# A four-layer encoder trunk: loading the memory in four parts, later placement of two waiting steps, and a last unit stored by token tile

## The reference, cut to what matters

```python
mem_n = rmsnorm(mem, mem_norm)                    # mem, x: 256 x 1024
for i in range(4):                                # kinds: SSM, DIFF, SGU, SSM
    h = rmsnorm(x, norm_mix[i])
    proj = h @ w_in[i]                            # last 1024 columns are the queries xq
    mix_out = mixer_i(proj[..., :-1024])          # mamba2 / differential attention / spatial gating
    k, v = split(mem_n @ w_mem_kv[i], 2)
    cross = softmax(rmsnorm_heads(xq) @ rmsnorm_heads(k).T / 16) @ v
    x = x + concat([mix_out, cross]) @ w_out[i]
    x = x + square(relu(rmsnorm(x, norm_ffn[i]) @ w_ff1[i])) @ w_ff2[i]
return x                                          # 256 x 1024
```

## Time and profile before

| what | value |
|---|---|
| median of 3 runs | 1874.03 us (1873.33 to 1874.39) |
| the profiled execution, its own time | 1873.39 us |
| its span in the profile | 1871.6 us |
| busy: PE, DVE, ACT, POOL | 1819.8, 1122.0, 1005.7, 241.3 us |
| mean granted TensorE clock | 0.99 |
| read from memory | 302.91 MB |

### The profile page before, as it was taken

The page is one execution under the profiler, slowest core; times in us unless marked ns, Lnnn a source line. Parts: engine busy times, 40 slices in busy tenths (PEclk is TensorE's granted clock), DMA queues, the critical chain, the costliest instruction groups (busy, mean ns, idle before and its releaser), DMA issues.

```text
span 1871.6 us, 27875 instructions
## 1 busy us (share of the span) xinstructions
PE 1819.8 (97%) x10596; PEld 1597.1 (85%) x10596; DVE 1122.0 (60%) x1492; ACT 1005.7 (54%) x1613; POOL 241.3 (13%) x581
## 2 busy tenths in 40 slices
PE   6999999999997899999999999999999999999998
PEld 5998878899986678899988888999799897889997
DVE  4877765565554575555556545555577776556554
ACT  5665765454454476454455655444555676545443
POOL 2132340000001131000002300000022144000000
PEclk8999999999998899999999999999999999999999
DMA  6444434555553343555556435555444444355553
GB/s 222 159 146 147 147 113 136 180 191 191 186 177 134 107 147 119 173 188 181 190 180 220 151 125 180 194 188 191 154 160 160 136 148 135 113 183 180 189 191 125
DMA packets 84161, 305.78 MB, mean 163 GB/s; under 512 B 9280, under 2 KB 9664, under 8 KB 84032
## 3 DMA queue, kind: packets, MB, share of 16 engines
q1 hardware_dynamic: 83744, 302.95, 48.7%
q10 hardware_dynamic: 288, 1.05, 0.1%
HBM read 302.91 MB, written 1.05 MB: 162 GB/s over the span
## 4 chain that ended last, share of the span: by engine, by line
PE 64%; DVE 2%; issue 2%; POOL 1%; ACT 1%; DVEq 0%; ACTq 0%
PE ps L1057 13%; PE ps L1059 12%; PE ps L1058 12%; PE ps L1066 6%; PE ps L1067 6%; PE ps L1068 6%; PE ps L1192 1%; PE ps L1212 1%; PE ps L1091 1%; PE ps L1083 1%; PE ps L1142 1%; DVE nt L1510 1%; PE ps L1120 1%; ACT nt L1305 0%; PE ps L1201 0%
## 5 line engine op out<-in xcount | busy, mean ns | idle before, releaser
L1453 DVE TENSOR_TENSOR w_lo_t<-raw,w_hi_t 128x1024 fp32r<-128x1024 f32 x570 | 704.2, 1239 | 514.8 <-ACT w_hi_t L1237 514.1
L1237 ACT ACTIVATE w_hi_t<-raw 128x1024 fp32r<-128x1024 f32 x570 | 601.6, 1060 | 433.8 <-PE ps L1059 200.8
L1066 PE MATMUL ps<-hT_hi,w_hi_t 128*128 128x256 f32 x1536 | 437.8, 285 | 0.0
L1068 PE MATMUL ps<-hT_hi,w_lo_t 128*128 128x256 f32 x1536 | 434.6, 283 | 0.0
L1067 PE MATMUL ps<-hT_lo,w_hi_t 128*128 128x256 f32 x1536 | 434.5, 283 | 0.0
L1057 PE MATMUL ps<-w_hi_t,act_hi 128*128 128x512 f32 x832 | 327.7, 394 | 0.0
L1058 PE MATMUL ps<-w_lo_t,act_hi 128*128 128x512 f32 x832 | 324.1, 390 | 0.0
L1059 PE MATMUL ps<-w_hi_t,act_lo 128*128 128x512 f32 x832 | 324.0, 389 | 0.0
L1067 PEld LDWEIGHTS ps<-hT_lo,w_hi_t 128*128 128x128 f32 x1536 | 294.6, 192 | 1.3
L1066 PEld LDWEIGHTS ps<-hT_hi,w_hi_t 128*128 128x128 f32 x1536 | 294.5, 192 | 1.4
L1068 PEld LDWEIGHTS ps<-hT_hi,w_lo_t 128*128 128x128 f32 x1536 | 294.5, 192 | 0.0
(11 more groups left out here) (191 smaller groups left out, 1967.9 us busy)
## 6 DMA issues: line engine op xcount, KB each, us to landing
raw<-in_wstream SPq DMA_DIRECT2D x570, 512.0 KB, 3.4
mix<-in_mem SPq DMA_DIRECT2D x1, 1024.0 KB, 5.2
x<-in_x SPq DMA_DIRECT2D x1, 1024.0 KB, 10.2
out<-x SPq DMA_DIRECT2D x2, 512.0 KB, 2.8
wsT<-in_sgu_wT ACTq DMA_DIRECT2D x1, 512.0 KB, 4.4
sgain<-in_sgu_gain ACTq DMA_DIRECT2D x1, 512.0 KB, 5.2
consts_sb<-in_consts SPq DMA_DIRECT2D x1, 384.0 KB, 11.2
percol_sb<-in_percol SPq DMA_DIRECT2D x1, 225.5 KB, 6.1
```

The costliest lines, as they stand in the source:

```text
L1066: pe.matmul(o, wh[:, n], ah, start=first and c == 0 and f % 2 == 0, stop=False, skip_group_check=True)
L1068: mm = pe.matmul(o, wl[:, n], ah, start=False, stop=last and c == UK - 1, skip_group_check=True)
L1237: act.activation(w_hi_t[:, u % RING, :], raw[:, u % RING, :], ACT.Copy).then_inc(w_hi, 1)
L1453: dve.tensor_tensor(w_lo_t[:, u % RING, :], raw[:, u % RING, :], w_hi_t[:, u % RING, :].bitcast(F32), ALU.subtract)\
```

## The change

The memory is loaded in four parts of 256 columns (each with a semaphore), issued between the first units; the gain of the memory's norm has a transfer of its own, and the rest of the per-column constants follows behind unit 3 in two transfers, which `setup` now waits for. In the planner the sums of squares and `rms` of the memory stand ahead of unit 0, and `x_norm` holds the sums of x and places `xn` 2 units after `rms`, and the turns 2 units after `xn`. `row_norm` places `nt_turn` 2 units after `norm_mul`. The last unit's `x_add` waits for each token tile by itself, and each is stored by itself (256 KB).

```diff
@@ row_norm
             self.step("norm_mul", job=job, groups=groups, r=r, n=n)
-            yield 1
+            yield 2
             for m in range(2):
                 tj = self.misc_job(True, False)
                 self.step("nt_turn", ...)
@@ build
-        def start():
-            yield 1
-            for nb in range(2):
-                self.sum_squares("mem", nb)
-            yield 1
-            self.r_m = self.rms("mem")
-            self.sum_squares("x", 0)
-            yield 1
-            self.sum_squares("x", 1)
-            yield 1
+        for nb in range(2):
+            self.sum_squares("mem", nb)
+        self.r_m = self.rms("mem")
+        def start():
+            yield 2
             yield from self.x_norm(0)
@@ x_norm
+        for nb in range(2):
+            self.sum_squares("x", nb, self.x_halves[nb])
         r = self.rms("x")
         n = self.count("xn")
-        yield 1
+        yield 2
         self.step("xn", n=n, rms=r)
-        yield 1
+        yield 2
@@ sync
+            mem_part(0)
             sp.dma_start(consts[:, 0:P], A["consts"][:, 0:P]).then_inc(ident_in, 16)
-            sp.dma_start(mix[:, :, D:2 * D], m_in).then_inc(mem_in, 16)
-            sp.dma_start(raw[:, 0, :], A["wstream"][0]).then_inc(raw_in[0], 16)
-            sp.dma_start(pc[:, :], A["percol"]).then_inc(pc_in, 16)
-            for u in range(1, RING):
-                sp.dma_start(raw[:, u, :], A["wstream"][u]).then_inc(raw_in[u], 16)
+            sp.dma_start(pc[:, g], A["percol"][:, g]).then_inc(gain_in, 16)
+            weights(0)
+            mem_part(1)
+            weights(1)
+            mem_part(2)
+            mem_part(3)
+            weights(2)
             sp.dma_start(x[:, :, :], x_rows).then_inc(x_in, 16)
+            weights(3)
+            sp.dma_start(pc[:, 0:g.start], ...).then_inc(pc_in, 16)
+            sp.dma_start(pc[:, g.stop:NPC], ...).then_inc(pc_in, 16)
...
+            for t in range(TT):
+                sp.wait_ge(tail_added, t + 1)
+                sp.dma_start(x_out[:, t, half:D], x[:, t, half:D]).then_inc(stored, 16)
@@ scalar and vector
+                if k == "setup":
+                    act.wait_ge(pc_in, 32)        # vector: the same wait
@@ vector, x_norm step
+                    if n:
+                        dve.wait_ge(x_pn, n)
@@ vector, x_add of the last unit
+                        if tail and t == 0:
+                            dve.wait_ge(tail_done, 1)
+                        elif tail:
+                            dve.wait_ge(job_done, job.done)
```

More of the change, by code:

```diff
@@ L342, in build @@
     def build(self):
-        self.turning, self.ready, self.v_act = False, {}, {}
+        self.turning, self.ready, self.v_act, self.x_halves = False, {}, {}, (0, 0)
         self.parts["mem"] = []
         for m in range(4):
-            self.parts["mem"].append(self.turn("mem", m, "memT", (2 * m, 2 * m + 1), (2 * m, 2 * m + 1), ("mem_norm", 2 * m), ("mem_in", 16)))
+            self.parts["mem"].append(self.turn("mem", m, "memT", (2 * m, 2 * m + 1), (2 * m, 2 * m + 1), ("mem_norm", 2 * m), (f"mem_in{m}", 16)))
             self.steps[-1]["w"] = m - AHEAD + 1
         self.step("setup")
+        for nb in range(2):
+            self.sum_squares("mem", nb)
+        self.r_m = self.rms("mem")
         def start():
-            yield 1
-            for nb in range(2):
-                self.sum_squares("mem", nb)
-            yield 1
-            self.r_m = self.rms("mem")
-            self.sum_squares("x", 0)
-            yield 1
-            self.sum_squares("x", 1)
-            yield 1
+            yield 2
             yield from self.x_norm(0)
-        self.r_m = 1
         self.spawn(start())
@@ L408, in into_x @@
         ub(b, 1, True, lambda: added(b, 1))
+        if what == "store":
+            self.steps[-2]["tail"] = self.steps[-1]["tail"] = True
         self.pair = b.banks[0] // 2
@@ L426, in rest @@
                 self.rms("x")
[L428 to L431, removed]
         if what == "turn":
@@ L436, in into_x @@
             self.parts["hT"] = []
-            self.spawn(scale_first(gain))
+            self.spawn(self.x_norm(gain))
         else:
@@ L854, in bass_trunk @@
         job_done, act_free, dve_free = sem("job_done"), sem("act_free"), sem("dve_free")
-        mem_in, ident_in, pc_in, consts_in, rows_in, x_in, stored = [sem(n) for n in ("mem_in", "ident_in", "pc_in", "consts_in", "rows_in", "x_in", "stored")]
+        ident_in, gain_in, pc_in, consts_in, rows_in, x_in, stored = [sem(n) for n in ("ident_in", "gain_in", "pc_in", "consts_in", "rows_in", "x_in", "stored")]
+        mem_in = [sem(f"mem_in{m}") for m in range(4)]
+        tail_done, tail_added = sem("tail_done"), sem("tail_added")
         act_chain, dve_chain = sem("act_chain"), sem("dve_chain")
@@ L921, in _ @@
                 sp.wait_ge(w_lo[plan.lo_on[u - RING]], plan.lo_n[u - RING])
-                sp.dma_start(raw[:, u % RING, :], A["wstream"][u]).then_inc(raw_in[u % RING], 16)
+                weights(u)
             x_out = out.rearrange("a (t p) d -> p (a t) d", p=P)
[L924 to L928, removed]
+            sp.wait_ge(dve_free, plan.x_halves[0])
+            sp.dma_start(x_out[:, :, 0:half], x[:, :, 0:half]).then_inc(stored, 16)
+            for t in range(TT):
+                sp.wait_ge(tail_added, t + 1)
+                sp.dma_start(x_out[:, t, half:D], x[:, t, half:D]).then_inc(stored, 16)
+            sp.wait_ge(stored, 48)
         @block.gpsimd
@@ L1059, in _ @@
                                 mm = pe.matmul(o, al, wh[:, n], start=False, stop=last and c == UK - 1)
+                            if s.get("tail") and t == 0:
+                                mm.then_inc(tail_done, 1)
                     elif s["form"] == "feat":
@@ L1267, in _ @@
                     if s["src"] == "mem":
-                        act.wait_ge(mem_in, 16)
+                        act.wait_ge(mem_in[2 * s["nb"]], 16)
+                        act.wait_ge(mem_in[2 * s["nb"] + 1], 16)
                     else:
@@ L1455, in lo_to @@
                     low[0] += 1
-            dve.wait_ge(pc_in, 16)
+            dve.wait_ge(gain_in, 16)
             for s in steps:
@@ L1698, in _ @@
                         dve.wait_ge(r_ffn_new, s["r"])
-                    dve.wait_ge(job_done, job.done)
+                    tail = s.get("tail")
+                    if not tail:
+                        dve.wait_ge(job_done, job.done)
                     for t in range(TT):
+                        if tail and t == 0:
+                            dve.wait_ge(tail_done, 1)
+                        elif tail:
+                            dve.wait_ge(job_done, job.done)
                         c = x[:, t, s["nb"] * COLS:(s["nb"] + 1) * COLS]
@@ L1705, in _ @@
                             ins = dve.tensor_tensor(c, ps[:, job.banks[t], :], c, ALU.add)
-                    ins.then_inc(dve_free, 1)
+                        if tail:
+                            ins.then_inc(tail_added, 1)
+                    if not tail:
+                        ins.then_inc(dve_free, 1)
             lo_to(NU)
```

15 lines of the change are left out of this document (12 added, 3 removed).

## The result

The changed kernel takes **1855.08 us** (median of 4 runs, 1852.4 to 1857.07), the kernel before 1873.74 us beside it (4 runs, 1873.33 to 1874.39). The ratio is 0.9901 [0.9885, 0.9916]: about 1% faster, and 7.1 us above the forecast of 1848, inside its range of 1835 to 1862. The profiled execution is the fastest of the four, 1852.4 us, where the sum of the terms gave 1847.0.

A forecast was written before the change was run, and what follows sets the result against it. PE, busy 97%, bounds the kernel; its weak places are 37.8 us of waits and 12.8 us of low clock. Gains less new waits sum to 26.4 us, giving 1847.0 profiled, 1848 us median, range 1835 to 1862.

The forecast's parts named there:

- Start: Kernel start to the turns of x: split loads, reordered sums and shorter waits together win 9.8 us.
- Unit 0: At the start: memory parts land earlier, so the first unit begins at 9.7 for 11.53, winning 1.8 us.
- Wait ahead of unit 3: At the start: late constants hold ACT's squares and the cast, a new PE wait of 2.0 us (0 to 5).
- Wait for the scaled x: At the start, ahead of the turns of x: 1.25 us for 8.42, too short for the clock to fall.
- Rival C: At the start: constants land at 16.9, unit 3 waits 4.6 us, clock falls; 1853 us, chance 0.08.
- First pair of layer 1: First two normed blocks of layer 1, no head thread yet: later nt_turn shrinks waits, winning 7.2 us.
- Second pair: Next two normed blocks of layer 1: nt waits shrink but d_turn waits appear, 2.6 us won (-5 to 11.2).
- The q, q, k, k blocks: Layer 1 blocks beside heads and group norm: new waits cost 4 us (0 to 15), small waits save 0.7.
- A: Layer 1: planner's load estimate keeps head steps apart from the norms, no collisions; 1835 us, chance 0.20.
- B: Layer 1: collisions spread, each early tick leaves a wait costing 5 us; 1861.5 us, chance 0.18.
- Layer 2 and the SSM layers: Layer 2's two waits shrink, winning 1.1 us; two small waits in the SSM layers go, 0.7 us.
- Rival D: All ten direct successions of normed blocks: later nt turning serialises engines, 5 us each; 1894 us, chance 0.03.

The follow-up runs named there:

- own tick: Changed kernel, but where normed blocks follow directly, only the norm's own thread is advanced early, not the heads' threads: 1843.08 us.
- whole loads: Changed kernel with the memory loaded in one transfer and the constants in one ahead of unit 1, as before the change: 1853.65 us.
- later setup: Changed kernel with only the norm's thread advanced early, and the constants' wait moved from ahead of the memory's squares to slot 2: 1839.41 us.
- second profile: The changed kernel run again without any edit, to show spread of waits and clock: 1856.87 us.
- single edits: Kernel before with only layer 3's scaled rows and turns later: 1864.69 us; kernel before with only the last unit added and stored by tile: 1871.89 us.
- values first: On top of the later setup, layer 1's first values block put ahead of its queries and keys: 1856.48 us.
- Shifting the phase by one slot: On top of values first, the heads started one slot later: 1839.39 us.
- later turn alone: Kernel before with nt_turn one unit later and the wait on x_pn this order needs, nothing else of the change: 1868.59 us.

## Why the prediction was right in sign and 7 us low

**Start, forecast 9.8, measured 6.2 in the profile.** Three of its terms were off.
- *Unit 0, +1.8 forecast.* The second part is turned at 7.64 for a landing forecast at 6.0, the third at 9.80 for 7.9. The step that failed is the rate of 2.45 us per MB, taken from landings of a queue that is already full. SP issues one transfer about every 0.5 us. The whole memory had gone out at 1.19 us; of the parts the second goes out at 2.67 and the last two only here:

```profile
3.66 1.36 SPq L911 DMA_DIRECT2D mix<-in_mem  x2
```

  The first stretches of each kernel (before, then changed; last column GB/s) show what was moved:

```profile
0.00:8.00 8.00, 1.50 (x7) 1.53 (x8) 0.00 (x0) 1.59 (x2) 0.20 (x4) 1.00 0.73 260
3.00:4.00 1.00, 0.00 (x0) 0.00 (x0) 0.00 (x0) 0.00 (x0) 0.00 (x0) 1.00 0.93 328
```

```profile
0.00:8.00 8.00, 1.47 (x6) 1.08 (x7) 0.88 (x2) 3.49 (x5) 0.20 (x4) 1.00 0.67 202
3.00:4.00 1.00, 0.22 (x1) 0.23 (x2) 0.00 (x0) 0.25 (x1) 0.00 (x0) 1.00 0.78 89
8.00:12.00 4.00, 2.96 (x14) 2.45 (x13) 3.49 (x5) 2.83 (x7) 0.00 (x0) 1.00 1.04 402
```

  In the first 8 us the split moved 58 GB/s less, 0.46 MB or 1.1 us at 410 GB/s; from 8 us on it ran at 402. Whether the issue times or the shorter rows of the parts did it, no run separates. By the rule of the Trainium skill that the prediction weighed ("DMA: Bandwidth & Descriptors", section Bandwidth: transfers of 1 MiB or more for 75% of peak) it had worked out that the parts' gain would be gone; the trace agrees in that. Unit 0 started at 11.42 for 11.53. On top, its first matmuls ran slowly:

```profile
11.42 0.78 PE L1070 MATMUL ps<-w_hi_t,memT_hi 128*128 128x512 f32 x1
12.00 0.63 PE L1071 MATMUL ps<-w_lo_t,memT_hi 128*128 128x512 f32 x1
...
13.70 0.41 PE L1072 MATMUL ps<-w_hi_t,memT_lo 128*128 128x512 f32 x1
```

  0.63 us is the length at the lower level (at 569.49 in the changed kernel it stands under a granted clock of 0.50); in the profile of before all after the first take 0.39 or 0.40. Unit 0's tenth matmul stands at 14.64 for 13.67. So this term was -1.0, not +1.8, and part of that is luck: the length of the slow start varies from one execution to the next (last section).
- *Wait ahead of unit 3, forecast 2.0, measured 0.97*: ACT did wait for the constants (2.74 us, until 16.32, where 14.3 was forecast), but unit 3 too came later.
- *Wait for the scaled x, forecast 1.25, measured 2.33*, for the same reason and one more: the memory's squares start later, POOL begins at 19.39 for 17.5, and its two chains take 5.8 and 6.0 us where 6.1 and 4.1 were forecast. The clock behind it stayed full, as forecast.

  The small waits of the stage won nothing: 0.74, 0.34, 0.37, 0.92 and 0.36 us before, 0.49, 0.92, 0.36 and a new one of 1.21 for the copy of `kT` after, 0.25 more, where 1.05 less was forecast. With 2.1 for the clock that is -1.0 - 1.0 + 6.1 + 2.1 - 0.25 = 5.95, and the stage shows 6.2. That the clock stayed full behind the 2.33 us was luck in part: with the own tick a wait of 2.34 us lowered it. The whole loads and the later setup tested it: each takes the wait ahead of unit 3 away and brings the output projection of layer 0 about 2.2 us forward. Rival C had the right cause: the constants came at 16.3, near its 16.9. But unit 3 waited 0.97 us, not 4.6, and the clock did not fall there; the slow matmuls ahead of 13.7 us stand before that wait and are not C's.

**First pair of layer 1, forecast 7.2: held.** Waits of 3.44 and 0.75 us and 4.0 x 0.35 = 1.4 us of clock behind the first, for 3.42, 0.5 and 1.6 forecast.

**Second pair, forecast 2.6: held, by terms that cancel.** The waits are 1.09, 1.78 and 3.71 us (forecast 1.1, 1.7 and 5.2; 4.97 in the second profile), `d_turn` being the step that waits in the last two. What was missing is the clock behind the first two: 4.0 x 0.50 + 4.0 x 0.24 = 3.0 us between 612 and 620. A wait of 1.19 us with full clock had stood for both, but here only the 1.07 us of transposes lie between the two. The third wait was 1.5 us shorter and the clock behind it cost 8.0 x 0.21 = 1.7 us for 2.9. Together 11.3 us for 13.5 before: 2.2 us won. The second profile gives 11.3 too, with 1.7 us of clock in place of the 3.0. That the unforeseen clock and the two smaller terms cancel is luck.

**The q, q, k, k blocks, forecast -4 + 0.7.** Waits of 1.52, 3.49 and 0.66 us and one under 0.2 for 1.0, 1.6 and 1.5: 5.8 us against 0.5 before, and, in the second profile, 3.2 us of clock. So they cost 5.3 or 8.5 us for 3.3. The size of the second wait and the chance of a low clock were not in the sum. This is nearly the whole miss of layer 1: 3.7 (profile) or 1.0 (second profile: 245.4 - 244.4) for 6.5.

**Between A and B.** The waits for `dS` are there, so A fell; two of them, not three, exceed 3 us, so B did not hold either, though the miss in these blocks has its sign. What the heads' moving up costs is what the own tick showed: without it layer 1 is 11.1 us shorter, and A's arrangement, made on purpose, gives 1843 us. A itself said 12.7 us below the forecast; the run is 12 to 14 below the changed kernel.

**Layer 2 and the SSM layers, forecast 1.1 and 0.7.** Layer 2 won 2.05. In the SSM layers the two waits of 0.37 and 0.38 us went as forecast, but in layer 3 a wait of 2.14 us for `dt_keep` stands where 0.73 and 0.35 us were, which no term had. Rival D counts four direct successions without a head thread; by the counts given with the kernel they are six (one in layer 0, the first in layer 1, three in layer 2, one in layer 3), which speaks against D still more.

**Layer 3 (7.1) and the end (1.2): held**, 7.3 us and 1.5 us as single edits. In the second profile of the changed kernel layer 3 won 6.0 us only, the clock having fallen behind the wait for `dt_keep`.

**From profile to median.** The forecast put the median 1 us above the profiled execution. It is 2.7 above: the profiled one had luck with the clock (at 681, and in layer 3). 5.4 us of the 7.1 are terms, the rest is this.

What stays open: which of the waits of 1 to 3.5 us lowers the clock. The same wait did and did not, and no run isolates it.

## What to carry to other kernels

Putting a step later to cover a wait is only half of the edit: look at what calls it early for a shared tile, and at who else that call moves. A short step on an in-order engine that falls behind a waiting one, with PE's next step depending on it, can cost more than the wait that was removed (values first: layer 1 took 246.0 us for 231.0). Shifting the phase by one slot took those 17 us back, though it gave no better median than the arrangement without the values first, so try the phase slot by slot. Cut a load into parts only after asking what is sent behind them and who waits for that; at the start the queue moved 89 GB/s between 3 and 4 us here, where it moved 402 from 8 us on.

## What the runs showed of the hardware

- **The clock at the start is not in the granted clock column.** It shows 1.00 from 8 to 12 us in the changed kernel, while 512-column matmuls take 0.63 us. Read the durations there. With the whole load the low level lasted at times too: the tenth matmul of unit 0 stood at 13.67 and 13.58 us in two profiles and at 15.54, 15.31 and 15.53 in three, behind the same 3.65 us of transposes; with the parts between 14.00 and 15.60. That is a lottery of 2 us, of which a later wait can take up most: in the kernel before and in that with the later turn alone the tenth matmul stood at 13.67 and 15.54, the turns of x behind the wait for the scaled rows at 36.53 and 37.02.
- **A wait of 3.49 us kept the full clock, one of 3.43 at the same place lost it**, and in layer 3 the same wait of about 2.1 us, which ends at 1365.80 and at 1369.09, left it at 1.00 in the changed kernel's first profile and at 0.83 over 10 us in its second:

```profile
1366.00:1376.00 10.00, 10.00 (x85) 10.00 (x85) 9.86 (x16) 6.24 (x8) 3.79 (x2) 1.00 0.51 160
```

```profile
1369.00:1379.00 10.00, 9.91 (x70) 9.94 (x71) 9.86 (x16) 5.02 (x7) 3.97 (x2) 0.83 0.50 160
```

- **POOL's small operations** take 0.19 us, or now and then 1.04 to 1.27 us for the same shape, so that the chain of `rms` took 5.8 and 6.0 us at the start of the changed kernel, with two long operations in each, and 4.1 us in the kernel before for the one that had none. These two stand in the changed kernel's timeline of POOL one behind the other:

```profile
20.49 0.19 POOL L963 TENSOR_TENSOR stats<-stats 128x2 f32<-128x2 f32 x1
20.77 1.04 POOL L964 TENSOR_SCALAR stats<-stats 128x2 f32<-128x2 f32 x1
```
